# PEER kernel on one core: V rows gathered for 64 tokens at a time and summed in two column halves of TensorE, norms moved to later slots, one-hots gated with two column scalars

## The reference, cut to what matters

```python
s1, i1 = lax.top_k(s[:, :, 0], PEER_TOPK)
s2, i2 = lax.top_k(s[:, :, 1], PEER_TOPK)
top, pos = lax.top_k(cand, PEER_TOPK)              # of the 16 x 16 sums
eidx = jnp.take_along_axis(cidx, pos, axis=-1)     # 8 x 16 experts a token
gate = jax.nn.softmax(top, axis=-1)
hid = gelu(einsum('td,thkd->thk', xb, take(u, eidx)))
out = einsum('thk,thkd->td', gate * hid, take(v, eidx))
x2 = LayerNorm(ALPHA * x1 + out)
```

## Time and profile before

| | |
|---|---|
| time, median of 3 runs | 3714.85 us (3713.38 to 3717.87) |
| time of the profiled execution | 3716.1 us |
| its span, first to last instruction | 3714.1 us |
| PE busy | 3371.2 us, 91% |
| DVE busy | 2674.5 us, 72% |
| POOL busy | 1708.9 us, 46% |
| ACT busy | 840.8 us, 23% |
| moved by DMA | 1083.39 MB, 292 GB/s on average |

### The profile page before, as it was taken

The page is one execution under the profiler, slowest core; times in us unless marked ns, Lnnn a source line. Parts: engine busy times, 40 slices in busy tenths (PEclk is TensorE's granted clock), DMA queues, the critical chain, the costliest instruction groups (busy, mean ns, idle before and its releaser), DMA issues.

```text
span 3714.1 us, 46046 instructions
## 1 busy us (share of the span) xinstructions
PE 3371.2 (91%) x15355; PEld 2344.4 (63%) x15355; DVE 2674.5 (72%) x5645; ACT 840.8 (23%) x1682; POOL 1708.9 (46%) x1424
## 2 busy tenths in 40 slices
PE   6998998899988999898987666799999999999998
PEld 6998997798733334343334434577767776777765
DVE  6662000588766899798898899677877777777777
ACT  2111111556501112121223333211111111111111
POOL 2332220122114666566664355455655555555553
PEclk9999999899989999999999988899999999999999
DMA  3333333667666999899997877999999999999997
GB/s 100 86 102 125 113 128 107 239 223 261 255 218 220 343 366 365 303 360 348 350 342 237 290 273 262 356 386 389 390 386 401 392 384 377 385 398 398 390 372 249
DMA packets 386635, 1083.39 MB, mean 292 GB/s; under 512 B 50160, under 2 KB 147408, under 8 KB 379264
## 3 DMA queue, kind: packets, MB, share of 16 engines
q0 software_dynamic: 186624, 679.56, 49.1%
q1 hardware_dynamic: 126616, 307.94, 23.1%
q10 hardware_dynamic: 73192, 93.41, 7.0%
HBM read 987.76 MB, written 93.02 MB: 291 GB/s over the span
## 4 chain that ended last, share of the span: by engine, by line
PE 45%; DVE 11%; DMA 8%; issue 6%; ACT 1%; POOL 1%; another core or an unknown queue 0%; SPq 0%; DVEq 0%; ACTq 0%; POOLq 0%
PE PB L1990 16%; PE PB L1977 13%; PE PB L2015 6%; PE PB L1953 5%; DMA x1d<-in_peer_u 3%; PE PB L1966 3%; DVE ub L1676 3%; DMA vbf<-in_peer_v,gix 2%; DVE oha L1620 1%; PE PB L2058 1%; DMA ub<-in_peer_u,gix 1%; PE PB L1935 1%; ACT stag L1821 1%; DVE ohb L1622 1%; DVE acc L1711 1%
## 5 line engine op out<-in xcount | busy, mean ns | idle before, releaser
L1408 POOL DMA_INDIRECT ub<-in_peer_u,gix x640 | 706.2, 1103 | 819.3 <-DVE hid L1676 587.0
L1408 POOL DMA_INDIRECT vbf<-in_peer_v,gix x640 | 734.5, 1148 | 366.3 <-issue 213.7
L1990 PE MATMUL PB<-vbd,wd 128*128 128x512 f32 x1536 | 684.2, 595 | 0.0
L2015 PE MATMUL PB<-vbf,dg 128*128 128x512 f32 x1020 | 527.9, 644 | 171.6 <-ACT dg L1858 129.3
L1977 PE MATMUL PB<-xds,uts 128*128 128x384 f32 x3072 | 568.6, 339 | 0.0
L1977 PEld LDWEIGHTS PB<-xds,uts 128*128 128x128 f32 x3072 | 530.8, 189 | 0.5 <-issue 0.5
L1676 DVE CUSTOM_DVE_ANT_0 ub<-ub,x1g 128x1024 f32<-128x1024 f32 x385 | 469.2, 1223 | 79.5 <-DMA ub<-in_peer_u,gix 49.3
L1990 PEld LDWEIGHTS PB<-vbd,wd 128*128 128x128 f32 x1536 | 283.7, 191 | 309.1 <-issue 309.1
L2015 PEld LDWEIGHTS PB<-vbf,dg 128*128 128x128 f32 x1020 | 194.7, 200 | 419.3 <-issue 256.7
L1636 DVE TENSOR_TENSOR uts<-PB,uts 128x512 fp32r<-128x512 f32 x256 | 175.9, 687 | 296.9 <-ACT uts L1834 288.4
L1711 DVE SCALAR_TENSOR_TENSOR acc<-vbf,wg,acc 128x1024 f32<-128x1024 f32 x257 | 329.0, 1280 | 12.7 <-DMA vbf<-in_peer_v,gix 11.5
(11 more groups left out here) (388 smaller groups left out, 5102.7 us busy)
## 6 DMA issues: line engine op xcount, KB each, us to landing
vbd<-in_peer_v SPq DMA_DIRECT2D x128, 512.0 KB
x1d<-in_peer_u SPq DMA_DIRECT2D x96, 512.0 KB
gd_d<-stag ACTq DMA_DIRECT2D x12, 2048.0 KB, 9.8
gbd<-gd_d SPq DMA_DIRECT2D x16, 1536.0 KB
ubd<-in_peer_u SPq DMA_DIRECT2D x32, 512.0 KB
wtr<-in_w_tok SPq DMA_DIRECT2D x12, 1024.0 KB, 8.2
tok_d<-stg ACTq DMA_DIRECT2D x96, 128.0 KB, 1.7
rb<-rows_d SPq DMA_DIRECT2D x8, 1536.0 KB, 8.5
```

The costliest lines, as they stand in the source:

```text
L1408: pool.indirect_dma_start(out=buf, out_offset=None, in_=a[table], in_offset=bass.IndirectOffsetOnAxis(ap=index, axis=0)).then_inc(done, 16)
L1990: last = T.matmul(PB[:, 2 * d + n, :], wd[:, b % 2, d * CH:(d + 1) * CH], vbd[b % 8][:, n * 512:(n + 1) * 512], start=b == 0, stop=b == NB ...
L2015: last = T.matmul(PB[:, x, :], dg[:, n % 2, :], vbf[:, v % NB, x * 512:(x + 1) * 512], start=v % CH == 0, stop=n_pe[v + 1] == n_pe[min((c ...
```

## The change

Five edits go together.

1. A V gather no longer brings one pick of 128 tokens. It brings two picks (ranks 2m and 2m+1) of 64 tokens: even rows `v` are for tokens 0 to 63, odd ones for tokens 64 to 127. The bytes are the same. The indices for this stand in new tiles `gixv`, which SP fills with four small DMAs a tile (16 for tile 0), and the weights in `wgv`, which SP fills after each head with four DMAs of 64 partitions x 8 floats (`turn_gates`). The stationary matrix is `fold` (two 64-wide identities, one above the other) scaled by a column of weights, so that a matmul sums the two picks of 64 tokens.
2. PE handles two rows at once, with four matmuls of 128 rows x 64 columns x 512; the first half of the array's columns goes to PSUM partitions 0 to 63, the second to 64 to 127. All V rows up to `PE_ROWS = 300` go to PE, none to DVE; they come `LAG_PE = 20` slots after their dot product, no longer 16. Rows 300 to 307 are done by DVE, two to a slot, in slots 320 to 323 (before, rows 304 to 307 were, one to a slot); from there on all is as before.
3. The norms of tiles 0 and 1 move from slots 144 and 272 to slots 258 and 278, behind the last norm of the first kind, so the vectors are loaded once for each kind. The accumulator of tiles 0 and 1 is the x1 buffer itself, preset of tiles 0 and 1 falls away, and `x1g[1]` has a buffer of its own, loaded at slot 64.
4. `one_hots` gates with `tensor_scalar` and two column scalars in place of `scalar_tensor_tensor` with a broadcast operand.
5. A few tiles of the pick share memory (`topv`, `gt`, `pa`).

```diff
-    LAG = TOPK
+    LAG, LAG_PE, SD = TOPK, TOPK + 4, 320
+    PE_ROWS = SD - LAG_PE
-    NORM2 = (144, 272, 400, 528)
-    ACC0 = {2: 0, 164: 1, 292: 2, 390: 3, 440: 4}
+    SUMS = (CH + LAG_PE, 2 * CH + LAG_PE)
+    NORM2 = (258, 278, 400, 528)
+    ACC0 = {302: 2, 390: 3, 440: 4}
...
+                def turn_gates(hv):
+                    sp.wait_ge(s["gate"], hv + 1)
+                    free(sp, s["diag"], 8 * (hv - 1))
+                    for e in range(2):
+                        for g in range(2):
+                            sp.dma_start(wgv[64 * e:64 * e + 64, hv % 2, 8 * g:8 * g + 8],
+                                         wg[64 * g:64 * g + 64, hv % 2, 8 * e:8 * e + 8]).then_inc(s_wgv[hv % 2], 16)
...
-                    if at == 8 and p < NP:
-                        sp.wait_ge(s["mulg"], p + 1)
-                        wide(gb1[:, :], "ln1_b", s["gl1"])
...
-                    if at == 12 and p + 1 < NP:
-                        sp.wait_ge(s["x1"], p + 1)
-                        wide(gb1[:, :], "ln1_g", s["gl1"])
...
-                        V.scalar_tensor_tensor(oha[:, q % 2, x, :], iof[:, :], it[:, d, 0, t0 + x:t0 + x + 1],
-                                               it[:, d, 2, t0 + x:t0 + x + 1].to_broadcast([P, P]), ALU.is_equal, ALU.mult)
+                        V.tensor_scalar(oha[:, q % 2, x, :], iof[:, :], it[:, d, 0, t0 + x:t0 + x + 1],
+                                        it[:, d, 2, t0 + x:t0 + x + 1], ALU.is_equal, ALU.mult)
...
+                            free(act, s["pv"], n - 1)
+                            for g in range(2):
+                                last = S.activation(dg[:, n % 2, g, :], fold[:, :], ACT.Copy, scale=wgv[:, hv % 2, 8 * g + m:8 * g + m + 1])
+                            last.then_inc(s["diag"], 1)
...
-                        for x in range(2):
-                            last = T.matmul(PB[:, x, :], dg[:, n % 2, :], vbf[:, v % NB, x * 512:(x + 1) * 512],
-                                            start=v % CH == 0, stop=n_pe[v + 1] == n_pe[min((c + 1) * CH, SD - LAG)])
+                            for x in range(2):
+                                for g in range(2):
+                                    last = T.matmul(PB[64 * g:64 * g + 64, x, :], dg[:, n % 2, g, :], vbf[:, (v0 + g) % NB, x * 512:(x + 1) * 512],
+                                                    start=v0 % CH == 0, stop=v + 1 == min((c + 1) * CH, PE_ROWS), tile_position=(0, 64 * g))
```

More of the change, by code:

```diff
@@ L1106, in background, with v_rows, by_dve @@
         return (0, s) if s < 24 else ((s + 12) // 36, (s + 12) % 36)
-    def by_pe(v):
-        s = v + LAG
-        if s >= SD:
-            return False
-        return not (s % 16 in (3, 8, 13) and (s < 144 or 168 <= s < 272 or 296 <= s))
-    n_pe = [0]
-    for v in range(U_SLOTS):
-        n_pe.append(n_pe[-1] + by_pe(v))
-    n_ax = [v - n_pe[v] for v in range(U_SLOTS + 1)]
+    def v_rows(t):
+        if t < LAG_PE:
+            return ()
+        if t < SD:
+            return (t - LAG_PE,)
+        if t < SD + LAG_PE - LAG:
+            v = PE_ROWS + 2 * (t - SD)
+            return (v, v + 1)
+        return (t - LAG,)
+    def by_dve(v):
+        return max(0, v - PE_ROWS)
     def parts_before(p):
@@ L1190, in build_peer @@
         gix = [sb(f"gix{n}", [P, 2, PH, TOPK]) for n in range(2)]
-        hid, wg = sb("hid", [P, 2, TOPK]), sb("wg", [P, 2, TOPK])
-        dg = sb("dg", [P, 2, P])
+        gixv = [sb(f"gixv{n}", [P, HK], u32)[:, :] for n in range(2)]
+        hid, wg, wgv = sb("hid", [P, 2, TOPK]), sb("wg", [P, 2, TOPK]), sb("wgv", [P, 2, TOPK])
+        dg, fold = sb("dg", [P, 2, 2, 64]), sb("fold", [P, 64])
         x1g_a, acc_a = sb("x1g", [P, D]), sb("acc", [P, D])
@@ L1200, in build_peer, with gates_of, pair_major @@
         x1s = (work[:, 0:D], work[:, D:2 * D], mt[:, :, :, :].rearrange("p a j t -> p (a j t)"), x1g_a[:, :], acc_b)
-        x1g = (x1g_a[:, :], x1g_a[:, :], x1g_b, x1g_a[:, :], x1g_b)
-        acc = (acc_a[:, :], acc_a[:, :], acc_a[:, :], acc_b, acc_a[:, :])
+        x1g = (x1g_a[:, :], acc_a[:, :], x1g_b, x1g_a[:, :], x1g_b)
+        acc = (x1g_a[:, :], acc_a[:, :], acc_a[:, :], acc_b, acc_a[:, :])
+        gixu = [g[:, 1, :, :].rearrange("p h k -> p (h k)").bitcast(u32) for g in gix]
+        def gates_of(p):
+            return res[:, 2, :, :] if p else gix[0][:, 0, :, :]
+        def pair_major(row):
+            return row.rearrange("p (a h m) -> p h m a", a=2, h=PH)
         s = {n: sem("pk_" + n) for n in (
@@ L1215, in build_peer @@
         s_gix = [sem(f"picks{n}") for n in range(2)]
+        s_gixv = [sem(f"v_picks{n}") for n in range(2)]
+        s_wgv = [sem(f"v_gates{n}") for n in range(2)]
         s_xg = [sem(f"x1g{n}") for n in range(2)]
@@ L1358, in _ @@
                         load_gix(3)
+                    if t >= TOPK and t % TOPK == 0 and t // TOPK <= (PE_ROWS + TOPK - 1) // TOPK:
+                        turn_gates(t // TOPK - 1)
                     if t == 300:
@@ L1541, in pick @@
                     step -= 1
+                    if (part, step) == (0, 0) and p >= 2:
+                        dve.wait_ge(s["pkst"], 16 * (p - 1))
                     if step < nh // 2:
@@ L1705, in _ @@
                             gated(b)
-                    if v >= 0 and not by_pe(v):
-                        dve.wait_ge(s_v[v % NB], 16 * (v // NB + 1))
-                        free(dve, s["ax"], n_ax[v])
-                        y = acc[v // CH]
-                        V.scalar_tensor_tensor(y, vbf[:, v % NB, :], wg[:, hv % 2, kv:kv + 1], y, ALU.mult, ALU.add).then_inc(s["ax"], 1)
+                    for v in v_rows(t):
+                        if v >= PE_ROWS:
+                            hv, col = v // TOPK, TOPK // 2 * (v % 2) + v % TOPK // 2
+                            dve.wait_ge(s_v[v % NB], 16 * (v // NB + 1))
+                            free(dve, s["ax"], by_dve(v))
+                            y = acc[v // CH]
+                            V.scalar_tensor_tensor(y, vbf[:, v % NB, :], wg[:, hv % 2, col:col + 1], y, ALU.mult, ALU.add).then_inc(s["ax"], 1)
                     for r in range(len(NORM2)):
@@ L1852, in _ @@
                         evac_scores(q, 3)
-                    if v >= 0 and by_pe(v):
-                        n = n_pe[v]
-                        if kv == 0:
-                            act.wait_ge(s["gate"], hv + 1)
-                        free(act, s["pv"], n - 1)
-                        S.activation(dg[:, n % 2, :], ident[:, :], ACT.Copy, scale=wg[:, hv % 2, kv:kv + 1]).then_inc(s["diag"], 1)
+                    for v in v_rows(t):
+                        if v < PE_ROWS and v % 2 == 0:
+                            n, hv, m = v // 2, v // TOPK, v % TOPK // 2
+                            if m == 0:
+                                act.wait_ge(s_wgv[hv % 2], 64 * (hv // 2 + 1))
+                            free(act, s["pv"], n - 1)
+                            for g in range(2):
+                                last = S.activation(dg[:, n % 2, g, :], fold[:, :], ACT.Copy, scale=wgv[:, hv % 2, 8 * g + m:8 * g + m + 1])
+                            last.then_inc(s["diag"], 1)
                     if q >= 2 and at == 0 and q <= NP:
```

197 lines of the change are left out of this document (100 added, 97 removed).

## The result

| | median | lowest to highest | runs |
|---|---|---|---|
| before | 3714.11 us | 3704.36 to 3717.87 | 4 |
| changed | 3659.79 us | 3655.92 to 3661.13 | 4 |

The ratio is 0.9856, 95% interval 0.9836 to 0.9876: 1.4% faster, where 95 us (2.6%) were forecast. The medians are 54.3 apart: the changed kernel was profiled in the fastest of its four runs.

A forecast was written before the change was run, and what follows sets the result against it. In slots 60 to 240 PE came first, DVE and DMA close behind; in 240 to 320 DVE set the pace. -49 - 18 - 28 = -95; 3716.1 - 95 - 1.25 = 3620 us, range 3580 to 3655, about 0.8 held up to 3722.

The forecast's parts named there:

- the rival of the ring: Slots 60 to 240: both gathers of a pair wait for the pair four slots back, 3.37 us a slot; 3674 us, chance 0.12.
- B: Slots 60 to 240, 601.1 us before: forecast 552 us, 49 less, set by DMA plus 12 us of waiting for U rows.
- C: Slots 240 to 320, 445.3 us before: 28 us less, from DVE work -9, PE and ACT's ring -25, one-hots +6.
- DVE's floor: Slots 60 to 240: DVE's busy time falls from 535.2 to 492 us, by 30 V-row passes and a norm.
- POOL's V gathers waiting for PE: Listed among the signs that would show the forecast wrong, without a size.
- A pair on PE: Two V rows on the array's halves take 5 steps, 2.15 us; PE then needs 474 us in slots 60 to 240.
- the rival of open loads: Weight loads no longer hidden under matmuls, 4.96 us a pair: 146 us slower, 3861 us, chance 0.10.
- the wait at slot 128: DVE's 8.6 us wait for x1g, where tile 1's x1 replaced tile 0's in one buffer, would go.
- the vectors' traffic: Slots 60 to 240: norm vectors no longer reloaded, 5.2 MB less, leaving 204 MB, 540 us at 378 GB/s.
- The gates: After each head, four small SP DMAs at 0.33 us, landed in 3 to 10 us, needed after 13.4: cost nothing.
- A: Slots 0 to 60, 232.1 us before: 18 us less, half of DVE's 36.3 us of waits; bounds 0 and 36.
- the port: DVE and GpSimd share a port; rival: all 384 one-hots lose 0.234 us, 90 us; 3704 us, chance 0.07.

The follow-up runs named there:

- half_by_half: Changed kernel with the order of a pair's four matmuls turned, both of one array half before both of the other; 3662.01 us, ratio 0.9859.
- lag24: Changed kernel with PE's V rows 24 slots behind their dot products in place of 20; 3660.48 us, ratio 0.9856.
- before_all_pe: Kernel before the change with all V rows up to slot 320 on PE, full width, one by one; 3745.72 us, ratio 1.0055.
- plain_norm_4buf: Changed kernel with the layer norms' gain and offset vectors left out and never loaded, still four V buffers; 3656.89 us, ratio 0.9834.
- plain_norm_5buf: As plain_norm_4buf, with five V buffers in place of four; 3593.11 us, ratio 0.9669.
- plain_norm_6buf: As plain_norm_4buf, with six V buffers in place of four; 3605.57 us, ratio 0.9701.

## Why the prediction held its sign and its range, and was 40 us too low

The measured 3659.8 us lie within the 3580 to 3722 stated, but past the 3655 that the forecast gave itself, and nearer to the rival of the ring (3674, chance 0.12) than to 3620. The sum was right that the gain would come from PE and DVE having less to do, and wrong on what would hold B then. C gave 10 us more than forecast, which hid a part of the miss in B.

**The failed step is the term for B, 49 us, of which 15 came.** The sum took the latest of three floors (PE 474, DVE 492, DMA 540) plus 12 us and gave the ring of V buffers no floor. DVE's floor was right: its busy time is 493. PE's work is 448 with the measured pair (280 + 90 x 1.87), lower still. DMA's 540 was reached once the ring was open, but that is partly luck, since PE has its part in the bound there. The four V buffers had a place above all three: 586 us. The ring's rival had 606 us. Three of its inputs were off. It took x1g's landing of 8.1 us for a gather's, which is 6.63 on average; it added that to three issues of POOL, though a landing is counted from the start of the issue, so that two belong in the sum (2.82 us with the 0.30 us of idle behind each, which it left out); and it had nothing between PE's end and POOL's start, 1.19 us. What would have led to a better chance: the ring's sum stood at 3.37 us a slot against 3.07 of the forecast, with bounds of the landing from 3.5 to 8.7 us; the forecast needed 6.9 or less every time, and a ring pays for each late landing, while nothing is paid back for an early one. A part of it is the clock: eleven pairs at the lower level make the average pair 0.18 us longer, 8 us over 45 turns. The prediction had looked at the granted clock in B as a matter of PE's busy time only.

The sign of failure "POOL's V gathers waiting for PE" came true, 44.3 us, and it was the one that mattered.

**A pair on PE.** Forecast 2.15 us, measured 1.87, so four steps and 0.15, not five. The premise of records that must follow the program's order was wrong (half_by_half). In B this is 25 us of PE's time, off the bound. That the halves overlap at all decided the sign: at 3.44 us the kernel is 0.9% slower than before. The Trainium skill, "TensorEngine Tiling (Array Packing)", Key Properties, has tiles work independently and in parallel, and a change of tiling mode drain the array. The trace agrees with the first; for the second, all that a pair costs beyond four steps is 0.15 us, and the 33 us that the prediction bounded for B would be 14 (90 x 0.15). The eight weight loads of a pair, 0.143 us each, are hidden in its 1.87 us, so that the rival of open loads falls. The Trainium skill, "TensorE: Matmul & The Clock Gate", The mechanism, has loads overlap matmuls in flight only when their row groups differ, but the same section also lets a load into the background weight buffer go ahead. Both halves use all rows, so the trace disagrees with the first and fits the second.

**DVE's floor, the wait at slot 128, the vectors' traffic.** 535.2 - 43.5 = 492 was measured as 493.2. No wait for x1g is left in B's groups. 202.9 MB went in B (586.4 us at 346 GB/s), forecast 204.

**The gates.** Covered, as said, but with two prices wrong: an issue on SP took 0.60 us and not 0.33, so four take 2.4, and with a median landing of 4.4 us a turn takes 6.8 us, inside the 3 to 10 of the forecast. ACT did wait at heads, 55 us in B, which the prediction had listed as a sign of failure; lag24 shows that it was none: without these waits B and the whole time stay.

**A** gave 14.1 of 18, but not in the way forecast. The 18 were half of the 36.3 us for which DVE waited. PE no longer waits for the first weights, yet DVE waits there 39.3 us for U rows:

```profile
DVE ub L1707 <- DMA ub<-in_peer_u,gix: 39.3, 15, 12.2
```

against 22.3 us. Its idle time of all kinds went from 47.0 to 43.4 us (232.1 - 185.1 and 218.0 - 174.6). Its busy time fell by 10.5 us, 10.2 of them the eight V rows that it summed in A before, a term that the sum had left out. before_all_pe takes the same rows off DVE and gains nothing in A, so it needs the cheap pairs or the lag as well; which of them is not isolated. That the number is near is luck. More buffers shorten slots 24 to 60 as well, from 138.1 us in plain_norm_4buf to 122.7 with six: the same ring.

**C** gave 38 of 28. DVE's busy time fell by 13.2 us (386.75 - 373.53) where 9 were forecast, its wait for PE's product by 27.9 where 25 were, and the 6 us set aside for the port were not needed: one-hots of 363 ns on average against the old form's 361. 13.2 + 27.9 = 41.1 us, 3 more than the stage gained. That the ring of PE and ACT opened is read from the waits and from the chain that ended last, and before_all_pe shows that C got longer with more in that ring; no run closed it again in the changed kernel. The granted clock in C fell from 0.89 to 0.81, while PE's busy time fell from 300.4 to 264.4 us. That it cost little is read from the chain, of which PE has 3.4%; no run shows it.

**What stays open.** What shares PE and DMA have in the 540 us of B with the ring open, and what brought the gain in A. What the complete kernel would do with five V buffers and four for U: no such version was run, for want of 4 KB in each partition. plain_norm_5buf, which leaves out gain and offset, at 3593 us, shows what that memory is worth: 61 us beside its control (0.9834 - 0.9669 = 1.65% of 3714). The 4.3 us by which slot 0 came later in the changed kernel's profile were not followed; other runs have slot 0 between 1079 and 1090 us.

## What to carry to other kernels

Floors of engines are not enough where buffers go round: write out the turn of each ring (release, issues, landing, use) for the gathers as they are grouped after the change, with the landing of that very kind of transfer, counted from where the profile counts it, and with its average or its upper part rather than its median. When consumers take two at a time, one odd buffer can be enough, since then only the second of a pair waits for the latest one; here the fifth gave all that the sixth did. A large wait in the trace is not the price of its cause: ACT's 55 us cost nothing, PE's 92 us gave back 42, and only a run without the cause tells which.

## What the runs showed of the hardware beside this

Matmuls on the two column halves of the array run side by side whatever their order in the program: 1.87 us for 8 records in both orders, and 3.44 us at full width. A DMA share of 0.95 did not mean that the DMA engines had 5% left: at that share they moved 346 to 348 GB/s, and at 0.99 they moved 375 with the same gathers, and 402 to 406 in windows of 30 us at 1.02 and 1.03 (plain_norm_6buf). Landing times rose meanwhile, from 6.4 to 7.0 us in the median (four and six buffers, V gathers of B). A DMA of 64 partitions x 8 floats within SBUF occupied SP's queue for 0.60 us, nearly double the 0.33 us of a vector's load, and took 4.4 us to land. After PE had stood for rows, pairs ran at a granted clock of 0.50 to 0.58 and took 3.2 to 3.7 us, and a buffer that waits for PE then comes free later too.
